# Expert weights handed over in order of use, loaded 2 MB and 4 MB at a time

## The chip, the cores and the metric

One Trainium2 chip, one core of it. The metric is the device time of one execution in microseconds; lower is better. The kernel before takes 1661.31 us (median of three runs, 1660.14 to 1664.47).

## The reference

A two-layer encoder trunk over 256 tokens of width 2048, all in float32. Layer 0 mixes tokens with a bidirectional mLSTM, layer 1 with multi-head latent attention. Each is followed by the same kind of expert stage, the part that the change touches:

```
gates = top 2 of the 4 experts of the best group, by sigmoid(x @ router_w)   # 16 experts, 4 groups
hg = x @ w_gate[e]          # (256, 2048) @ (2048, 512), for every expert e
hu = x @ w_up[e]            # the same shape
a  = silu(hg) * hu * gates[:, e]
y += a @ w_down[e]          # (256, 512) @ (512, 2048)
```

All 16 experts of a layer are read: 3 x 4 MB each, 201 MB a layer, 403 MB in all, out of some 534 MB that the whole kernel loads.

## The kernel before

**Stages.** Layer 0's mixer runs until about 414 us of the profiled span, its expert stage to 849 us, layer 1's mixer to 1217 us and its expert stage to the end.

**Units, pairs, steps.** Expert weights are counted in units of 1 MB: 128 partitions x 4 rows x 512 columns of float32, 8 KB in each partition. Experts are worked on in 8 pairs a layer; a pair has 24 units, numbered k = 24 i + n within the layer. TensorE multiplies both experts of a pair in turns, one in each half of the array, so that a step of 16 matmuls needs one unit of each expert: a pair is 12 steps, 8 of gate and up (L1173) and 4 of down (L1218). Units n = 0 to 15 are gate and up, 16 to 23 are down. The last pair's down projection goes by columns (L1237), from a tensor that the host lays out for it (`in_last_down`), units k = 184 to 191.

**The order within a load.** A load is one expert's 2 MB: 16 KB in a row for each partition, which is two units of the same expert. Units 0 and 1 are therefore expert e = 0, and 2 and 3 expert e = 1, while a step takes units 0 and 2, the next 1 and 3. The function `in_turn(k)` gives the place in the order of use: k // 4 * 4 + (0, 2, 1, 3)[k % 4].

**Places.** There are 23 places of 8 KB a partition for the first 23 units, and 18 of them are used again in a ring: `seat(k)` is (k - 4) % 18 for k from 34 on, and 0 to 10 for k = 23 to 33. A place of the first 23 units is one of 0 to 22; units 18 and 19 sit in 16 and 17, unit 22 in 11, and places 18 to 22 are not used again. `DOUBLE[s]` is the tile of two neighbouring places, s even. The last pair's units go to places of their own order (176 to 183 to 0 to 7, 184 to 191 to 10 to 17).

**The queue of loads.** SyncE issues all weight loads, in program order, on one queue. Before each it waits (`room`, L581) until the semaphore `unit_used` says that what was in the place has been multiplied; TensorE raises it by one for each unit, in the order of use. The loop at L633 issues the units k = 23 to 55 (`FINE` = 56) one by one, 1 MB each, sorted by when their place comes free; the loop at L636 issues k = 56 to 167 in order by 2 MB; the last pair's come by 1 MB again (L645), and its last two up units, 13 and 15 (`LAST_UPS`), by halves. Line 590 of the profile is `single` (1 MB), line 587 is `double` (2 MB).

**Waits of TensorE.** `arrived(n)` waits for the landing of unit n's load: for 2 MB loads at each even n.

Of the kernel before, what the change touches and what calls it, by code (L numbers as in the profile page):

```python
# [112 lines left out]
FINE = 56  # L113
# [3 lines left out]
LAST_UPS = (13, 15)  # L117


def in_turn(k):  # L120

    return k if k >= BY_COLUMNS else k // 4 * 4 + (0, 2, 1, 3)[k % 4]


def seat(k):


    if k >= BY_COLUMNS:
        return k - BY_COLUMNS + RING + 2
    if k >= BY_COLUMNS - RING:  # L130
        return k - BY_COLUMNS + RING
    if k == ALONE:
        return WIDE + ONCE
    if k == WIDE + ONCE:
        return ALONE
    if EARLY <= k < EARLY + ALONE:
        return k - EARLY
    return k if k < WIDE - 2 else k + 2 if k < WIDE else k - 2 if k < WIDE + 2 else k if k < EARLY else (k - ONCE) % WIDE
# [12 lines left out]
def split(u):  # L151

    k, singles = (u - U_MOE0, SINGLES[0]) if u < U_CKV else (u - U_MOE1, SINGLES[1])
    return expert(u) and (k in singles or k >= PAIRS * PAIR_UNITS - HALVES)


def places():

    slots, turns, held = [], [], [0] * EARLY

    for u in range(U_ALL):
        if u < U_MOE0:
            s = u % RING
        elif u < U_CKV:
            s = seat(u - U_MOE0)
        elif u < U_MOE1:
            s = (u - U_CKV) % RING
        else:
            k = seat(u - U_MOE1)
            s = (k + U_MOE1 - U_CKV) % RING if k < RING else k  # L170
        if not expert(u) or s % 2 == 0 or split(u):
            held[s] += 1
        slots.append(s)
        turns.append(held[s])
    return slots, turns
# [67 lines left out]
def trunk(nc, w, out):  # L243
# [8 lines left out]
    with ctx:  # L252
# [38 lines left out]
        DOUBLE = {}  # L291
        ring, LO = [], []
        for s in range(RING):
            here = top[0]
            if s % 2 == 0:
# [5 lines left out]
        DOUBLE[RING + 8] = sb("SPARE", [P, 2, UNIT_K, UNIT_C])  # L301
# [168 lines left out]
        def in_double(u):  # L470

            if PLACE[u] == WIDE + ONCE:
                return UNIT_ALONE[:, :, :]
            return DOUBLE[PLACE[u] // 2 * 2][:, PLACE[u] % 2, :, :]

        def gate_rows(layer):

            return (w[n][layer].rearrange("e (q p k) f -> e q p (k f)", p=P, k=2 * UNIT_K)
                    for n in ("moe_w_gate", "moe_w_up"))

        def down_rows(layer):

            return w["moe_w_down"][layer].rearrange("e (c p k) d -> e c p (k d)", p=P, k=2)

        def half(v, k):

            return v[:, UNIT_K * UNIT_C * k:UNIT_K * UNIT_C * (k + 1)]

        def expert_sources(wg, wu, wd, i):

            n, h = divmod(i, 2) if isinstance(i, int) else i
            for q in range(2):
                for m in (wg, wu):
                    for e in range(2):
                        yield m[PER_GRP * (2 * h + e) + n, q]
            for c in range(2):
                for e in range(2):
                    yield wd[PER_GRP * (2 * h + e) + n, c]
# [13 lines left out]
        def _(sp):  # L512
            used = sem("unit_used")

            def unit(u, src, i=0):
                if U_CKV <= u < U_CKV + RING:
                    sp.wait_ge(used, U_MOE0 + in_turn(last_in(PLACE[u])) + 1)
# [51 lines left out]
            def spare(layer, base):  # L569

                u = base + WIDE
                if layer:
                    sp.wait_ge(used, U_MOE0 + in_turn(last_in(PLACE[u] + 1)) + 1)
                src = list(expert_sources(*gate_rows(layer), down_rows(layer), 0))[WIDE // 2]
                sp.dma_start(flat4(DOUBLE[PLACE[u]]), src).then_inc(sem(f"unit_loaded_{PLACE[u]}"), 16)

            def experts(layer, base):
                wg, wu = gate_rows(layer)
                wd = down_rows(layer)

                def room(k, units):  # L581

                    last = max(in_turn(before_in_slot(k + n)) for n in range(units))
                    sp.wait_ge(used, base + last + 1)
# [8 lines left out]
                first = list(expert_sources(wg, wu, wd, 0))  # L593
# [29 lines left out]
                single(base + WIDE + ONCE, list(expert_sources(wg, wu, wd, 0))[(WIDE + ONCE) // 2])  # L623
# [8 lines left out]
                all_of = [src for i in range(PAIRS) for src in expert_sources(wg, wu, wd, i)]  # L632
                for k in sorted(range(EARLY, FINE), key=lambda k: in_turn(before_in_slot(k))):  # L633
                    room(k, 1)
                    single(base + k, all_of[k // 2])
                for i in range(PAIRS):  # L636
                    if i == MIDDLE:
                        sp.wait_ge(sem("over_done"), layer + 1)
                    for n in range(PAIR_UNITS // 2):
                        k = PAIR_UNITS * i + 2 * n  # L640
                        if FINE <= k < PAIRS * PAIR_UNITS - HALVES:
                            room(k, 2)
                            double(base + k, all_of[k // 2])
                front = PAIRS * PAIR_UNITS - PAIR_UNITS
                for k in sorted(range(PAIRS * PAIR_UNITS - HALVES, PAIRS * PAIR_UNITS), key=in_turn):  # L645
                    room(k, 1)
                    if k >= BY_COLUMNS:
                        d, c = divmod(k - BY_COLUMNS, 2)
                        sp.dma_start(in_double(base + k).rearrange("p k c -> p (k c)"), w["last_down"][layer, d, c])\
                            .then_inc(sem(f"unit_loaded_{PLACE[base + k]}"), 16)  # L650
                    elif k - front not in LAST_UPS:
                        single(base + k, all_of[k // 2])
                    elif k - front == LAST_UPS[-1]:
                        for h in range(2):
                            for n in LAST_UPS:
                                src = half(all_of[(front + n) // 2], n % 2)
                                rows = slice(2 * h, 2 * h + 2)
                                sp.dma_start(in_double(base + front + n)[:, rows, :].rearrange("p k c -> p (k c)"),
                                             src[:, 2 * h * UNIT_C:2 * (h + 1) * UNIT_C])\
                                    .then_inc(sem(f"unit_loaded_{PLACE[base + front + n]}" if h else "last_ups_begun"), 16)  # L660
# [40 lines left out]
            sp.wait_ge(used, U_MOE0 + max(in_turn(last_in(RING + n)) for n in range(2)) + 1)  # L701
# [28 lines left out]
        def _(pool):  # L730
# [7 lines left out]
            for l in range(2):  # L738
# [14 lines left out]
                wg, wu = gate_rows(l)  # L753
                wd = down_rows(l)
                with pool.If(flag > 0):
                    with pool.Fori(0, EXTRA) as q:
                        with pool.Fori(0, PER_GRP) as i:
                            with pool.Fori(0, 2) as h:
                                j = q * PAIRS + 2 * i + h
                                whole = list(expert_sources(wg, wu, wd, (i, h)))  # L760
                                srcs = [half(whole[2 * b + e], k) for b in range(PAIR_UNITS // 4) for k in range(2) for e in range(2)]
# [10 lines left out]
        def _(pe):  # L772
# [284 lines left out]
            def experts(l, base):  # L1057
                def order(n):

                    return n // 4 * 4 + 2 * (n % 2) + n // 2 % 2  # L1060

# [69 lines left out]
                def opening(m, g, arrived, slot, consumed, left_out=()):  # L1131
# [3 lines left out]
                    arrived(2)  # L1135
                    for c in range(UNIT_K):
                        for e in range(2):
                            last = pe.matmul(PS[64 * e:64 * e + 64, 0, :], tokens_of(c, e),
                                             slot(2 * e)[:, c, :], start=(c == 0), stop=False)
# [6 lines left out]
                def pair(m, j, g, following, arrived, slot, consumed, whole, prev, first=False, opened=False, late=False):  # L1146
# [7 lines left out]
                    for q in range(2):  # L1154
                        if first:
                            gather_some(m, g, (2 * q, 2 * q + 1), True)
                        for up in range(2):
                            for k in range(2):
                                if first and up == 0:
                                    pe.wait_ge(sem(m + "xg_ready"), 4 * g + 2 * q + k + 1)  # L1160
                                units = [8 * q + 4 * up + 2 * e + k for e in range(2)]
                                here = not (opened and q == up == k == 0)
                                in_two = whole and not following and units[0] == LAST_UPS[0]
                                if in_two:
                                    pe.wait_ge(sem("last_ups_begun"), 32 * (l + 1))
# [44 lines left out]
                    for c in range(FC):  # L1210
                        units = [16 + 4 * (c // 2) + 2 * e + c % 2 for e in range(2)]
# [40 lines left out]
                def overflow():  # L1252
# [3 lines left out]
                    with pe.Fori(0, EXTRA) as q:  # L1256
                        with pe.Fori(0, PAIRS) as i:
                            k = q * PAIRS + i
                            j, g = k + MIDDLE + LAYER_PAIRS * l, k + MIDDLE + 1 + LAYER_GATHERS * l
                            for d in range(4):  # L1260
# [3 lines left out]
                            pair(m, j, g, 0, lambda n: pe.wait_ge(sem(f"over_loaded_{l}_{order(n) % 4}"),  # L1264
                                                                  16 * (PAIR_UNITS // 4) * k + 16 * (order(n) // 4 + 1)),
                                 lambda n: OV[order(n) % 4], sem(f"over_free_{l}"), False, False)
# [555 lines left out]
        def _(dve):  # L1822
# [718 lines left out]
_WEIGHTS = ["x", "a_w_in", "a_w_out", "b_w_in", "b_w_ukv", "b_q_norm", "b_k_norm", "b_w_out",  # L2541
            "moe_w_gate", "moe_w_up", "moe_w_down"]
# [61 lines left out]

# [14 lines left out]
```

## Time and profile before

| | |
|---|---|
| median of three runs | 1661.31 us |
| the profiled execution's own time | 1661.03 us |
| its span | 1659.3 us |
| TensorE busy | 1611.1 us, 97% of the span |
| VectorE, ScalarE, GpSimd busy | 46%, 29%, 3% |
| loads and stores | 535.84 MB, mean 323 GB/s |
| mean granted TensorE clock | 0.996 of full speed |

The span runs from the first to the last instruction; the execution's own time lies 1.7 us above it. TensorE is nearly always busy, yet a share over the whole span says nothing of a single stage: in the expert stages the profile shows the DMA engines at 9 tenths or more in every slice, with 412 to 429 GB/s, and in the mixers at 150 to 300 GB/s. Issue to landing is the time from SyncE's issue of a load to its semaphore; where it is many times the duration of the transfer, the load has stood behind others.

### The profile page before, as it was taken

To read this page: it belongs to the slowest core of one execution; us is meant where nothing else is said; L and a number is where in the kernel's file an instruction comes from. 1 tells how busy PE (TensorE), PEld (TensorE's weight loads), DVE (VectorE), ACT (ScalarE), POOL (GpSimd) and SP (SyncE) were. 2 spreads that over 40 slices of the span, in tenths; PEclk is the share of its full clock that TensorE was granted. 3 is DMA by queue.
4 is the path that set the end of the run, shared out by engine and by line. 5 is a ranking of instruction groups with operands and counts; after the bars stand their busy time and mean duration, and the time that the engine had idled before them with its cause. 6 is when DMAs were issued, how large, how long until landed. Compare 5 with 4: busy or idle time off the path is not lost.

```text
span 1659.3 us, 19405 instructions
## 1 busy us (share of the span) xinstructions
PE 1611.1 (97%) x8014; PEld 1010.1 (61%) x8014; DVE 758.6 (46%) x1316; ACT 482.1 (29%) x622; POOL 44.9 (3%) x26
## 2 busy tenths in 40 slices
PE   9999999999999999889999999999999999989898
PEld 8888888887433434333459999888754344333343
DVE  5885477744332222212267777684532322222223
ACT  6444456434000000000054565564320000000000
POOL 0000000000000000000040000020000000000000
PEclk9999999999999999999999999999999999999999
DMA  9755656577999999999995545554799999999998
GB/s 368 268 189 166 198 166 197 171 264 298 421 415 425 428 427 427 428 429 425 420 360 174 152 137 158 190 179 151 290 423 421 423 427 428 428 427 428 427 422 342
DMA packets 110441, 535.84 MB, mean 323 GB/s; under 512 B 8704, under 2 KB 28048, under 8 KB 77840
## 3 DMA queue, kind: packets, MB, share of 16 engines
q1 hardware_dynamic: 109920, 534.04, 82.0%
q8 instruction: 66, 1.08, 0.3%
q10 hardware_dynamic: 432, 0.53, 0.1%
q14 instruction: 23, 0.19, 0.0%
HBM read 532.43 MB, written 2.11 MB: 322 GB/s over the span
## 4 chain that ended last, share of the span: by engine, by line
PE 81%; DMA 15%; DVE 2%; ACT 1%; SPq 1%; issue 1%; DVEq 0%; ACTq 0%
PE PS L806 33%; PE PS L1173 21%; PE PS L1218 8%; DMA DOUBLE<-in_moe_w_down 5%; DMA DOUBLE<-in_moe_w_up 5%; PE PS L927 2%; PE PS L1079 2%; DMA SPARE<-in_moe_w_gate 2%; PE PS L1237 2%; DMA OVD<-in_moe_w_gate 2%; PE PS L1116 2%; PE PS L1117 1%; PE PS L933 1%; DMA ring<-in_a_w_in 1%; PE PS L1099 1%; PE PS L1004 1%
## 5 line engine op out<-in xcount | busy, mean ns | idle before, releaser
L1173 PE MATMUL PS<-DOUBLE,AREA 128*64 128x512 f32 x1264 | 336.1, 597 | 10.8 <-DMA OVD<-in_moe_w_gate 5.4
L1834 DVE TENSOR_TENSOR LO<-ring,HI 128x2048 fp32r<-128x2048 f32 (+1 forms) x122 | 262.4, 2151 | 168.1 <-ACT HI L1459 167.6
L806 PE MATMUL PS<-HI,XT_BOTH 128*128 128x512 f32 (+1 forms) x1344 | 298.0, 373 | 1.1 <-issue 0.6
L1459 ACT ACTIVATE HI<-ring 128x2048 fp32r<-128x2048 f32 (+1 forms) x122 | 219.8, 1802 | 272.4 <-PE PS L806 234.5
L806 PEld LDWEIGHTS PS<-HI,XT_BOTH 128*128 128x128 f32 x1344 | 244.1, 188 | 35.5 <-issue 2.4
L1173 PEld LDWEIGHTS PS<-DOUBLE,AREA 128*64 128x64 f32 x1264 | 107.6, 139 | 196.0 <-issue 195.7
L1173 PE MATMUL PS<-OVD,AREA 128*64 128x512 f32 x400 | 179.2, 599 | 0.0
L806 PE MATMUL PS<-LO,XT_BOTH 128*128 128x512 f32 (+1 forms) x672 | 152.5, 368 | 0.0
L2243 DVE TENSOR_TENSOR AREA<-PS,SMALL 128x512 f32<-128x512 f32 x64 | 44.1, 689 | 236.3 <-PE PS L1079 203.0
L1218 PE MATMUL PS<-DOUBLE,AREA 128*64 128x512 f32 x528 | 143.4, 599 | 3.6 <-DMA DOUBLE<-in_moe_w_down 3.2
L1645 ACT ACTIVATE AREA<-PS 128x512 f32<-128x512 f32 x16 | 9.6, 597 | 438.7 <-PE PS L1173 438.7
L806 PEld LDWEIGHTS PS<-LO,XT_BOTH 128*128 128x128 f32 x672 | 122.9, 188 | 16.2
L2233 DVE TENSOR_TENSOR X<-PS,X 128x512 f32<-128x512 f32 x112 | 69.9, 682 | 122.1 <-PE PS L1117 122.1
L1655 ACT ACTIVATE Y_hi<-PS,AREA 128x512 fp32r<-128x512 f32 x64 | 44.0, 688 | 229.4 <-PE PS L1218 197.7
L2251 DVE SCALAR_TENSOR_TENSOR Y_lo<-PS,AREA,Y_hi 128x512 fp32r<-128x512 f32 x64 | 48.0, 750 | 107.1 <-ACT Y_hi L1655 102.3
L1218 PEld LDWEIGHTS PS<-DOUBLE,AREA 128*64 128x64 f32 x528 | 45.6, 137 | 69.3 <-issue 66.2
L1173 PEld LDWEIGHTS PS<-OVD,AREA 128*64 128x64 f32 x400 | 54.2, 139 | 44.2 <-issue 44.2
L1173 PE MATMUL PS<-SPARE,AREA 128*64 128x512 f32 x176 | 78.4, 593 | 0.5 <-DMA DOUBLE<-in_moe_w_gate 0.5
L1173 PE MATMUL PS<-WIDED,AREA 128*64 128x512 f32 x160 | 72.2, 596 | 0.8 <-DMA OVD<-in_moe_w_up 0.8
L1079 PEld LDWEIGHTS PS<-AREA,XN 128*128 128x128 f32 x448 | 47.9, 140 | 34.0 <-issue 34.0
L1218 PE MATMUL PS<-OVD,AREA 128*64 128x512 f32 x144 | 63.9, 595 | 3.3 <-DMA WIDED<-in_moe_w_down 3.3
L1079 PE MATMUL PS<-AREA,XN 128*128 128x128 f32 x448 | 61.2, 280 | 0.0
(325 smaller groups left out, 1847.3 us busy)
## 6 DMA issues: line engine op xcount, KB each, us to landing
DOUBLE<-in_moe_w_up SPq DMA_DIRECT2D x26, 2048.0 KB, 24.3
DOUBLE<-in_moe_w_gate SPq DMA_DIRECT2D x24, 2048.0 KB, 21.4
DOUBLE<-in_moe_w_down SPq DMA_DIRECT2D x24, 2048.0 KB, 28.5
ring<-in_a_w_in SPq DMA_DIRECT2D x47, 1024.0 KB, 5.2
DOUBLE<-in_moe_w_gate SPq DMA_DIRECT2D x30, 1024.0 KB, 13.3
DOUBLE<-in_moe_w_up SPq DMA_DIRECT2D x24, 1024.0 KB, 15.1
ring<-in_b_w_in SPq DMA_DIRECT2D x32, 768.0 KB, 4.4
OVD<-in_moe_w_up SPq DMA_DIRECT2D x9, 2048.0 KB, 29.1
```

Source lines behind the costliest of these rows:

```text
L806: mm = pe.matmul(PS[:, banks[t], 0:n], lhs(k0 + kk, t)[part], weights[:, kk, 0:n], start=first and kk == 0 and p == 0, stop=last and kk == ...
L927: pe.matmul(PS[:, 4 * (b % 2) + ch, :], HI[u % 2][:, kk, ch * P:(ch + 1) * P], XT_BOTH[:, :, k, :], start=k == 0, stop=False)
L1079: last = pe.transpose(PS[:, GATHER_BANKS[g] + k // 2, at_:at_ + P], XN[:, t, c * P:(c + 1) * P], m_["SEL"][:, t, :])
L1116: pe.matmul(PS[:, bank, :], SCT[:, t * P:(t + 1) * P], YH[:, d, :], start=True, stop=False)
L1173: last = pe.matmul(PS[64 * e:64 * e + 64, up, :], tokens_of(c, e), slot(units[e])[:, kk, :], start=(c == 0), stop=(c == DC - 1))
L1218: last = pe.matmul(PS[64 * e:64 * e + 64, 4 + d, :], m_["AT"][:, c, 64 * e:64 * e + 64], slot(units[e])[:, d, :], start=(c == 0), stop=(c ...
L1459: act.activation(HI[s % 2][:, :, 0:n], ring[PLACE[u]][:, :, 0:n], ACT.Copy).then_inc(sem("hi_ready"), 1)
L1655: act.activation(YH[:, d, :], PS[:, 4 + d, :], ACT.Copy, scale=m_["GS"])\
L1834: tt(LO[PLACE[u]][:, :, 0:n], ring[PLACE[u]][:, :, 0:n], HI[s % 2][:, :, 0:n], ALU.subtract)\
L2233: tt(xs, PS[:, bank, :], xs, ALU.add).then_inc(sem(counted), 1)
L2243: tt(m_["XG"][:, 4 * g:4 * g + 4, :].rearrange("p k (t s) -> p k t s", t=NT), PS[:, banks[g]:banks[g] + 2, :].rearrange("p b (k t s) -> p ...
L2251: stt(YL[:, d, :], PS[:, 4 + d, :], m_["GS"], YH[:, d, :], ALU.mult, ALU.subtract)\
```

## The change

The host lays out the expert weights in one tensor, `in_experts`, of shape (2 layers, 8 pairs, 6 blocks, 128 partitions, 32 KB). A block is four units in order of use: (first half, e = 0), (first half, e = 1), (second half, e = 0), (second half, e = 1). Two units that are used in one step are neighbours, in memory and in the place. `in_turn` is gone; the three expert tensors are no longer inputs. The bytes that are loaded, the matmuls and their order stay.

Pairs 4, 5 and 6 (k = 96 to 167) are loaded by 4 MB: 32 KB in a row for each partition, into four tiles of four neighbouring places, in turn. Their places 8 and 9 stay unused in these pairs. The tile SPARE moves to lie behind HI, so that one of the four is in one piece. `FINE` goes from 56 to 34: units 34 to 55 are loaded by 2 MB, in order, and not by 1 MB as places come free. Of the last pair, gate and up come by 2 MB (units 168 to 181), the last two ups still in two halves, now 1 MB for both experts together.

```diff
-FINE = 56
+FINE = 34
-LAST_UPS = (13, 15)
-def in_turn(k):
-    return k if k >= BY_COLUMNS else k // 4 * 4 + (0, 2, 1, 3)[k % 4]
+LAST_UPS = (14, 15)
+QUAD_PAIRS = (4, PAIRS - 1)
+QUAD_SEATS = ((4, 5, 6, 7), (12, 13, 14, 15), (10, 11, 16, 17), (0, 1, 2, 3))
+def quad(k):
+    return QUAD_PAIRS[0] * PAIR_UNITS <= k < QUAD_PAIRS[1] * PAIR_UNITS

 def seat(k):
+    if quad(k):
+        return QUAD_SEATS[(k - QUAD_PAIRS[0] * PAIR_UNITS) // 4 % 4][k % 4]
...
-        DOUBLE = {}
+        DOUBLE, QUAD = {}, {}
+        DOUBLE[RING + 8] = sb("SPARE", [P, 2, UNIT_K, UNIT_C])
+        QUAD[RING + 4] = at("QUADX", over_at - 2 * UNIT_K * UNIT_C * 4, [P, 4, UNIT_K, UNIT_C])
+        QUAD[RING + 2] = at("QUADH", over_at + 2 * UNIT_K * UNIT_C * 4, [P, 4, UNIT_K, UNIT_C])
...
+        def two_units(layer, i, n):
+            return half(w["experts"][layer, i, n // 2], 2 * (n % 2), 2)
...
                 def room(k, units):
-                    last = max(in_turn(before_in_slot(k + n)) for n in range(units))
+                    last = max(before_in_slot(k + n) for n in range(units))
                     sp.wait_ge(used, base + last + 1)
...
-                for k in sorted(range(EARLY, FINE), key=lambda k: in_turn(before_in_slot(k))):
+                for k in sorted(range(EARLY, FINE), key=before_in_slot):
                     room(k, 1)
                     single(base + k, all_of[k // 2])
                 for i in range(PAIRS):
...
-                        if FINE <= k < PAIRS * PAIR_UNITS - HALVES:
+                        if quad(k):
+                            if k % 4 == 0:
+                                room(k, 4)
+                                sp.dma_start(flat4(QUAD[PLACE[base + k]]), w["experts"][layer, i, n // 2])\
+                                    .then_inc(sem(f"unit_loaded_{PLACE[base + k]}"), 16)
+                        elif FINE <= k < PAIRS * PAIR_UNITS - HALVES:
                             room(k, 2)
                             double(base + k, all_of[k // 2])
...
-                for k in sorted(range(PAIRS * PAIR_UNITS - HALVES, PAIRS * PAIR_UNITS), key=in_turn):
+                for k in range(PAIRS * PAIR_UNITS - HALVES, BY_COLUMNS, 2):
+                    room(k, 2)
+                    if k - front != LAST_UPS[0]:
+                        double(base + k, all_of[k // 2])
...
-                                units = [8 * q + 4 * up + 2 * e + k for e in range(2)]
+                                units = [8 * q + 4 * up + 2 * k + e for e in range(2)]
...
-                        units = [16 + 4 * (c // 2) + 2 * e + c % 2 for e in range(2)]
+                        units = [16 + 2 * c + e for e in range(2)]
...
+def expert_rows(inputs):
+    gate, up, down = (np.asarray(inputs[n]) for n in ("moe_w_gate", "moe_w_up", "moe_w_down"))
+    rows = np.empty((2, PAIRS, PAIR_UNITS // 4, P, 2, 2, UNIT_K * UNIT_C), np.float32)
+    for i in range(PAIRS):
+        n, h = divmod(i, 2)
+        for e in range(2):
+            x = PER_GRP * (2 * h + e) + n
+            for q in range(2):
+                for at, a in ((2 * q, gate), (2 * q + 1, up), (4 + q, down)):
+                    rows[:, i, at, :, :, e] = a[:, x].reshape(2, 2, P, 2, -1)[:, q]
+    return rows.reshape(2, PAIRS, PAIR_UNITS // 4, P, 4 * UNIT_K * UNIT_C)
```

## Rows read from the trace of the kernel before

**Rows 1.** The page: its span, and its DMA row by slices.

```profile
span 1659.3 us, 19405 instructions
DMA  9755656577999999999995545554799999999998
```

**Rows 2.** Busy time by window, layer 1's pairs 2-3 and 4-5; columns named in the first row.

```profile
core 0: us, PE busy (x) PEld busy (x) DVE busy (x) ACT busy (x) POOL busy (x), PEclk, DMA share, GB/s
1358.00:1410.00 52.00, 51.57 (x254) 20.98 (x252) 13.79 (x25) 4.33 (x7) 0.00 (x0) 1.00 1.01 427
1462.00:1514.00 52.00, 46.17 (x218) 19.05 (x218) 12.24 (x21) 3.35 (x5) 0.00 (x0) 1.00 1.01 427
```

**Rows 3.** The chain that ended last, layer 1's expert stage: start, us, what.

```profile
1478.39 31.91 DMA DOUBLE<-in_moe_w_up
...
1517.52 31.93 DMA DOUBLE<-in_moe_w_up
...
1558.90 30.20 DMA DOUBLE<-in_moe_w_down
...
1589.23 7.09 PE PS L1218 x32
...
1608.70 15.21 DMA DOUBLE<-in_moe_w_up
```

**Rows 4.** The same chain, the end of layer 0's expert stage and what follows.

```profile
756.07 30.53 DMA DOUBLE<-in_moe_w_down
...
786.73 8.79 PE PS L1218 x32
...
818.07 10.58 PE PS L1173 x48
...
849.65 1.90 ACT HI L1459
```

**Rows 5.** SyncE's issues in time, layer 0; the last row is layer 1's counterpart.

```profile
455.48 3.76 SPq L590 DMA_DIRECT2D SPARE<-in_moe_w_up  x2
...
463.52 0.33 SPq L590 DMA_DIRECT2D OVD<-in_moe_w_gate  x1
...
470.35 0.80 SPq L590 DMA_DIRECT2D DOUBLE<-in_moe_w_down  x2
...
473.78 0.81 SPq L590 DMA_DIRECT2D DOUBLE<-in_moe_w_down  x2
...
479.26 0.80 SPq L590 DMA_DIRECT2D DOUBLE<-in_moe_w_down  x2
...
484.89 0.33 SPq L590 DMA_DIRECT2D DOUBLE<-in_moe_w_down  x1
...
1267.19 0.33 SPq L590 DMA_DIRECT2D OVD<-in_moe_w_gate  x1
```

**Rows 6.** Issue to landing of single loads, by tile: three issues of layer 0.

```profile
L590 SPq DMA_DIRECT2D OVD<-in_moe_w_up x1: 431/431/431, 449.6 to 449.6; - x1
DMA to landing us min/median/max: 15.0/15.0/15.0
...
L590 SPq DMA_DIRECT2D SPARE<-in_moe_w_up x1: 328/328/328, 458.9 to 458.9; - x1
DMA to landing us min/median/max: 10.7/10.7/10.7
...
L590 SPq DMA_DIRECT2D DOUBLE<-in_moe_w_down x2: 327/380/432, 470.3 to 470.7; - x2
DMA to landing us min/median/max: 6.7/7.7/8.8
```

**Rows 7.** Issue to landing of two 2 MB loads that met an idle queue.

```profile
L587 SPq DMA_DIRECT2D DOUBLE<-in_moe_w_gate x1: 328/328/328, 381.5 to 381.5; - x1
L587 SPq DMA_DIRECT2D DOUBLE<-in_moe_w_up x1: 327/327/327, 393.4 to 393.4; - x1
...
DMA to landing us min/median/max: 8.1/8.4/8.7
```

More of the change, by code:

```diff
@@ L153, in split, with in_quad @@
     k, singles = (u - U_MOE0, SINGLES[0]) if u < U_CKV else (u - U_MOE1, SINGLES[1])
-    return expert(u) and (k in singles or k >= PAIRS * PAIR_UNITS - HALVES)
+    return expert(u) and (k in singles or k >= BY_COLUMNS)
+def in_quad(u):
+    return expert(u) and quad(u - U_MOE0 if u < U_CKV else u - U_MOE1)
 def places():
@@ L170, in places @@
             s = (k + U_MOE1 - U_CKV) % RING if k < RING else k
-        if not expert(u) or s % 2 == 0 or split(u):
+        if in_quad(u):
+            held[s] += 1 if u % 4 == U_MOE0 % 4 else 0
+        elif not expert(u) or s % 2 == 0 or split(u):
             held[s] += 1
@@ L294, in trunk @@
             here = top[0]
+            if s % 4 == 0:
+                QUAD[s] = at(f"QUAD{s}", here, [P, 4, UNIT_K, UNIT_C])
             if s % 2 == 0:
@@ L300, in trunk @@
         DOUBLE[WIDE + 2] = at(f"DOUBLE{WIDE + 2}", x_at, [P, 2, UNIT_K, UNIT_C])
-        DOUBLE[RING + 8] = sb("SPARE", [P, 2, UNIT_K, UNIT_C])
         SMALL = sb("SMALL", [P, SMALL_W])
@@ L473, in in_double, with half @@
                 return UNIT_ALONE[:, :, :]
+            if in_quad(u):
+                return QUAD[PLACE[u - (u - U_MOE0) % 4]][:, (u - U_MOE0) % 4, :, :]
             return DOUBLE[PLACE[u] // 2 * 2][:, PLACE[u] % 2, :, :]
[L476 to L498, printed above, removed]
+        def half(v, k, n=1):
+            return v[:, UNIT_K * UNIT_C * k:UNIT_K * UNIT_C * (k + n)]
+        def two_units(layer, i, n):
+            return half(w["experts"][layer, i, n // 2], 2 * (n % 2), 2)
         def stream(s):
@@ L516, in unit @@
                 if U_CKV <= u < U_CKV + RING:
-                    sp.wait_ge(used, U_MOE0 + in_turn(last_in(PLACE[u])) + 1)
+                    sp.wait_ge(used, U_MOE0 + last_in(PLACE[u]) + 1)
                 elif u >= RING:
@@ L572, in spare @@
                 if layer:
-                    sp.wait_ge(used, U_MOE0 + in_turn(last_in(PLACE[u] + 1)) + 1)
-                src = list(expert_sources(*gate_rows(layer), down_rows(layer), 0))[WIDE // 2]
-                sp.dma_start(flat4(DOUBLE[PLACE[u]]), src).then_inc(sem(f"unit_loaded_{PLACE[u]}"), 16)
+                    sp.wait_ge(used, U_MOE0 + last_in(PLACE[u] + 1) + 1)
+                sp.dma_start(flat4(DOUBLE[PLACE[u]]), two_units(layer, 0, WIDE // 2)).then_inc(sem(f"unit_loaded_{PLACE[u]}"), 16)
             def experts(layer, base):
-                wg, wu = gate_rows(layer)
-                wd = down_rows(layer)
                 def room(k, units):
-                    last = max(in_turn(before_in_slot(k + n)) for n in range(units))
+                    last = max(before_in_slot(k + n) for n in range(units))
                     sp.wait_ge(used, base + last + 1)
@@ L591, in single @@
                         .then_inc(sem(f"unit_loaded_{PLACE[u]}"), 16)
-                first = list(expert_sources(wg, wu, wd, 0))
+                first = [two_units(layer, 0, n) for n in range(PAIR_UNITS // 2)]
                 def early(k):
@@ L622, in experts @@
                 early_half(11)
-                single(base + WIDE + ONCE, list(expert_sources(wg, wu, wd, 0))[(WIDE + ONCE) // 2])
+                early_half(WIDE + ONCE)
                 if layer == 0:
@@ L631, in experts @@
                 early(WIDE + 2)
-                all_of = [src for i in range(PAIRS) for src in expert_sources(wg, wu, wd, i)]
-                for k in sorted(range(EARLY, FINE), key=lambda k: in_turn(before_in_slot(k))):
+                all_of = [two_units(layer, i, n) for i in range(PAIRS) for n in range(PAIR_UNITS // 2)]
+                for k in sorted(range(EARLY, FINE), key=before_in_slot):
                     room(k, 1)
@@ L644, in experts @@
                 front = PAIRS * PAIR_UNITS - PAIR_UNITS
-                for k in sorted(range(PAIRS * PAIR_UNITS - HALVES, PAIRS * PAIR_UNITS), key=in_turn):
-                    room(k, 1)
[L647 to L660, printed above, removed]
+                for k in range(PAIRS * PAIR_UNITS - HALVES, BY_COLUMNS, 2):
+                    room(k, 2)
+                    if k - front != LAST_UPS[0]:
+                        double(base + k, all_of[k // 2])
+                    else:
+                        src = all_of[k // 2].rearrange("p (e k) -> p e k", e=2)
+                        for h in range(2):
+                            rows = slice(2 * h, 2 * h + 2)
+                            sp.dma_start(DOUBLE[PLACE[base + k]][:, :, rows, :].rearrange("p e k c -> p e (k c)"),
+                                         src[:, :, 2 * h * UNIT_C:2 * (h + 1) * UNIT_C])\
+                                .then_inc(sem(f"unit_loaded_{PLACE[base + k]}" if h else "last_ups_begun"), 16)
+                for k in range(BY_COLUMNS, PAIRS * PAIR_UNITS):
+                    room(k, 1)
+                    d, c = divmod(k - BY_COLUMNS, 2)
+                    sp.dma_start(in_double(base + k).rearrange("p k c -> p (k c)"), w["last_down"][layer, d, c])\
+                        .then_inc(sem(f"unit_loaded_{PLACE[base + k]}"), 16)
             a_in = k_view(w["a_w_in"][0])
@@ L700, in _ @@
                 unit(U_CKV + n, b_in[n][:, :, Q_COLS:Q_COLS + RANK])
-            sp.wait_ge(used, U_MOE0 + max(in_turn(last_in(RING + n)) for n in range(2)) + 1)
+            sp.wait_ge(used, U_MOE0 + max(last_in(RING + n) for n in range(2)) + 1)
             sp.dma_start(b_["WKR"], w["b_w_in"][0].rearrange("(c p) n -> p c n", p=P)[:, :, Q_COLS + RANK:])\
@@ L752, in _ @@
                 flag = pool.value_load(FLAG[0:1, l:l + 1], min_val=0, max_val=1)
-                wg, wu = gate_rows(l)
-                wd = down_rows(l)
                 with pool.If(flag > 0):
@@ L759, in _ @@
                                 j = q * PAIRS + 2 * i + h
-                                whole = list(expert_sources(wg, wu, wd, (i, h)))
-                                srcs = [half(whole[2 * b + e], k) for b in range(PAIR_UNITS // 4) for k in range(2) for e in range(2)]
+                                srcs = [half(two_units(l, 2 * i + h, n // 2), n % 2) for n in range(PAIR_UNITS)]
                                 for n, src in enumerate(srcs):
@@ L1057, in experts @@
             def experts(l, base):
-                def order(n):
-                    return n // 4 * 4 + 2 * (n % 2) + n // 2 % 2
                 def gather(m, j, groups=range(4), first=False, chunks_of=range(4), low_of=None):
@@ L1134, in opening @@
                     arrived(0)
-                    arrived(2)
+                    arrived(1)
                     for c in range(UNIT_K):
@@ L1138, in opening @@
                             last = pe.matmul(PS[64 * e:64 * e + 64, 0, :], tokens_of(c, e),
-                                             slot(2 * e)[:, c, :], start=(c == 0), stop=False)
+                                             slot(e)[:, c, :], start=(c == 0), stop=False)
                             if c == UNIT_K - 1:
@@ L1164, in pair @@
                                 if in_two:
-                                    pe.wait_ge(sem("last_ups_begun"), 32 * (l + 1))
+                                    pe.wait_ge(sem("last_ups_begun"), 16 * (l + 1))
                                 for n in units if here and not in_two else ():
@@ L1263, in overflow @@
                             gather_some(m, g)
-                            pair(m, j, g, 0, lambda n: pe.wait_ge(sem(f"over_loaded_{l}_{order(n) % 4}"),
-                                                                  16 * (PAIR_UNITS // 4) * k + 16 * (order(n) // 4 + 1)),
-                                 lambda n: OV[order(n) % 4], sem(f"over_free_{l}"), False, False)
+                            pair(m, j, g, 0, lambda n: pe.wait_ge(sem(f"over_loaded_{l}_{n % 4}"),
+                                                                  16 * (PAIR_UNITS // 4) * k + 16 * (n // 4 + 1)),
+                                 lambda n: OV[n % 4], sem(f"over_free_{l}"), False, False)
                     gather(m, gather_turn(l, MIDDLE), (0, 1))
@@ L2538, in _ @@
             experts(1)
-_WEIGHTS = ["x", "a_w_in", "a_w_out", "b_w_in", "b_w_ukv", "b_q_norm", "b_k_norm", "b_w_out",
-            "moe_w_gate", "moe_w_up", "moe_w_down"]
+_WEIGHTS = ["x", "a_w_in", "a_w_out", "b_w_in", "b_w_ukv", "b_q_norm", "b_k_norm", "b_w_out"]
 def constants():
@@ L2602, in laid_out @@
     }
+def expert_rows(inputs):
+    import numpy as np
+    gate, up, down = (np.asarray(inputs[n]) for n in ("moe_w_gate", "moe_w_up", "moe_w_down"))
[8 more added lines that the diff above has]
+    return rows.reshape(2, PAIRS, PAIR_UNITS // 4, P, 4 * UNIT_K * UNIT_C)
 def kernel(**inputs):
@@ L2612 @@
     arrays.update(laid_out(inputs))
+    arrays["in_experts"] = expert_rows(inputs)
     arrays["in_last_down"] = down_blocks(inputs)
```

## The prediction, made before the result was known

> **What bounds the kernel now.** I read the page first: TensorE is busy for 97% of the span, but the DMA row shows two stretches of nines, and these are the expert stages [rows 1]. So the second view is busy time by window. In layer 1's pairs 2 to 3 TensorE works for 51.57 of 52 us and the DMA engines show a share of 1.01 at 427 GB/s; in pairs 4 to 5 the DMA row is the same and TensorE is down to 46.17 us [rows 2]. The loads never pause, TensorE does: a pair's 24 MB take longer to arrive than to be multiplied, the 23 units loaded ahead are used up by the fourth pair, and from there the stage goes at the pace of the queue.
>
> The third view, the chain, gives that pace. The long waits in layer 1 end with landings: 1478.39 + 31.91 = 1510.30, then 1549.45, 1589.10 and 1608.70 + 15.21 = 1623.91 [rows 3]. By the order of units these are the landings of the unit counts 136, 152, 168 and 182 (count 136: units 0 to 135 are there). 136 to 152 is 8 loads of 2 MB in 39.15 us: 4.89 us each, back to back. 168 to 182 is 14 loads of 1 MB in 34.81 us: 2.49 us each, so 4.97 for two. The waits also stand in layer 0, where the chain ends at 756.07 + 30.53 = 786.60 (count 168) [rows 4]. The rest of each stage hangs on these landings. What counts is thus only when the DMA queue delivers units 168 to 184; a TensorE wait taken away earlier comes back later.
>
> **Two units in order instead of four out of order.** A step now needs one 2 MB load and not two. In pairs 1 to 3 no wait on a load stands in the chain, so nothing is gained there; in pairs 4 to 6 a load is 4 MB, and the count that must have landed is again a multiple of four; in the last pair two 1 MB loads in turn order were as fine as one 2 MB load is. Price 0. It could only be worth something if the queue had slack, and it has none [rows 2]. The new order of freeing is the same too: before, units 0 and 2 came free in one step, now 0 and 1.
>
> **1 MB loads become 2 MB loads.** Units 34 to 55 are 11 pairs of loads, 168 to 181 are 7. Each saves 4.97 - 4.89 = 0.08 us of the queue: 0.9 us before count 168 and 0.6 us after it, in each layer.
>
> **2 MB loads become 4 MB loads.** 18 a layer. No row shows one. From 8 KB to 16 KB a row the queue won 0.08 us on 2 MB; if a row of any length costs the same extra, 4 MB win 0.08 us again: 9.70 for 9.78. That gives 18 x 0.08 = 1.5 us a layer. Bounds: 0 if the row of 16 KB is already at the port's pace, 3 us if the saving per load doubles instead, and 1.5 us of loss if one long row blocks as much as it saved before. I take 1.5, the value nearest to the row. The Trainium skill, DMA: Bandwidth & Descriptors, "Where 436 GB/s comes from", gives 435.2 GB/s as the ports' ceiling; by it 4 MB take no less than 9.64 us and the 18 loads could save 2.6 us at most. The trace, at 428.8 GB/s for 2 MB, agrees with a ceiling close by.
>
> The four tiles are refilled when their own four units are used. The tightest is the second, units 100 to 103, whose places were last held by units 88 to 91. TensorE uses unit 24 at 470.35 [rows 5] and needs at most 52 us a pair [rows 2], so unit 91 is used by about 470.35 + 67 / 24 x 52 = 615.5; count 100 lands at 786.60 - 34 x 4.89 = 620.3 at the earliest, later by the hole below. The issue comes in time, and later ones lie further ahead. Nothing is lost there.
>
> **FINE = 34, the term that goes the other way.** Before, the single loads follow whatever place comes free. Look at the issues between 455 and 471 us [rows 5]: unit 38 at 455.48, 39 at 458.92 (both SPARE), unit 51 at 463.52 (place 11, freed by unit 22, far ahead of its turn), then unit 40, and 41 and 43 at 470.35. After the change, units 38 and 39 go as one load at 458.92, when place 17 is free. The next in order is the load of units 40 and 41 into places 0 and 1. Place 0 held unit 23, place 1 unit 24, and 24 is used in the first step of pair 1 only: the issue of 470.35 [rows 5]. Unit 51 waits for its neighbour 50. So between 458.92 and 470.35 nothing is issued.
>
> How full is the queue then? The issue of 449.6 (count 38) lands at 464.6, that of 458.9 (count 40) at 469.6, and the two of 470.3 and 470.7 (43 and 44) at 477.0 and 479.5 [rows 6]: 2.49 us apart throughout, so the queue before just held, with the last landing 4 us behind the issue. After: count 38 lands at 464.4 (two of its loads are 2 MB now), count 40 at 469.3, and the queue is empty a microsecond before anything new is issued. A 2 MB load that met an idle queue took 8.1 to 8.7 us to land [rows 7]. So count 42 lands at 470.35 + 8.4 = 478.75 where a full queue would give 469.3 + 4.9 = 474.2: a hole of 4.5 us. The next loads are issued at 473.8, 479.3 and 484.9 [rows 5], while the queue then holds to 483.6 and 488.5; with 8.4 us each they make it, the last one barely. After that the places are aligned and issues run ahead. Bounds: 1.1 us if a start from idle cost nothing, 5.5 us if the first is 8.7 and the load of 484.9 slips by 0.7. The Trainium skill, the same page, "Anatomy of one DMA", gives a lone DMA 2.0 us plus bytes over 436 GB/s, 6.8 us for 2 MB; by it the hole would be 3.0 us. The two rows at 8.1 and 8.7 differ from it, though measured beside other work.
>
> Can it be caught up? No: the queue has no slack afterwards [rows 2, 3]. Layer 1 issues at the same distance (1267.19 for 463.52, pair 0 being 803.67 us later) [rows 5], so it has the same hole.
>
> **The sum.** Count 168 lands later by 4.5 - 0.9 - 1.5 = 2.1 us in each layer. In layer 1 the ups of the last pair bind (count 182), 0.6 us earlier: +1.5. In layer 0 the 32 matmuls after the wait take 8.79 us where layer 1 shows 7.09 [rows 3, 4], and TensorE comes to the ups at 818.07 + 10.58 / 3 = 821.6, 34.9 us after the landing, against 34.2 for seven 2 MB loads: TensorE binds, and layer 0 is +2.1. ScalarE's first split of the next stage (849.65) follows at once [rows 4], so the shift is handed on. Together +3.6 us on the profiled execution's 1661.03 (span 1659.3): 1664.6. The median of the runs is 1661.31, 0.3 higher; I say 1664.9.
>
> **Rivals.** A change under 0.3% (5 us) can't be told from none for this kernel.
>
> (a) No hole: the queue is fuller than my ledger says, or it restarts at no cost. For it: the before is seamless at the same place, and 1.1 us is a possible price. Against: 11.4 us without an issue with 4 MB queued. Then layer 0 wins 0.9 + 1.5 and layer 1 3.0: -5.4 us, 1655.9, faster. 20%.
>
> (b) The slow side: 4 MB loads bring nothing, since 16 KB rows are at the port's pace, and the hole stands. It costs 1.5 us more in each layer: +6.6, 1667.9. It decides from the point where a 4 MB load takes more than about 9.74 us. For it: nothing in the trace shows a faster pace than 429 GB/s. Against: the step from 1 MB to 2 MB did gain. The Trainium skill, the same page, "Rules for kernel authors", is content with 1 MB a DMA for full bandwidth; the trace's 0.08 us between 1 and 2 MB is small but there. The same time comes out if the hardware cuts the 32 KB rows in two. 28%.
>
> (c) The finer order does let TensorE through: if half of TensorE's idle time of the last three pairs of both layers went, by the window of pairs 4 to 5 (52 - 46.17) x 6 / 2 = 17 us [rows 2], the time would be 1644. Against it stands the DMA share of 1.01 while TensorE waits [rows 2]. 5%.
>
> My forecast with its own bounds (1661 to 1667.5) has 47%.
>
> Range 1655.5 to 1669.5: it takes in (a) and (b), and leaves out (c) and a hole of over 5 us together with lossy 4 MB loads. Faster by over 0.3%: 19% (14 of (a), all of (c)); slower: 35% ((b), and 7 of the forecast, its upper edge); same: 46%.
>
> **What would show it.** Right: by window, a DMA share well under 1 around 469 to 473 us and 1273 to 1277 us; an issue gap at SyncE from 458.9 to 470.35; one landing of 8 to 9 us there with nothing before it; landings 9.70 us apart in pairs 4 to 6; the last wait on ups ending near 1627.5 us in layer 1. Wrong: a DMA share of 1.01 in these windows, or 9.78 us and more for 4 MB, or TensorE idle before the ups gone.

## The result, and the profile after

The changed kernel takes 1664.65 us (median of 19 runs) beside 1661.88 us for the kernel before (19 runs in the same sessions): a ratio of 1.0017, 95% interval 1.001 to 1.0025, so 2.8 us slower. That is within what I had called no change, but with 19 runs the interval leaves out 1: the loss is small and real. The forecast was 1664.9. The profiled execution's span is 1662.2 us, 2.9 us more than before [rows 1]; its page:

```profile
span 1662.2 us, 19256 instructions
DMA  9755656577989999999995545554799999999998
```

The DMA row is the one of before [rows 1] but for one digit: slice 12 (457 to 499 us) has an 8 where there was a 9. By window (columns as in [rows 2]), layer 0 and then layer 1:

```profile
460.00:466.00 6.00, 6.00 (x31) 2.08 (x31) 1.22 (x2) 1.08 (x2) 0.00 (x0) 1.00 1.01 429
466.00:472.00 6.00, 6.00 (x30) 2.02 (x28) 2.76 (x6) 1.67 (x3) 0.00 (x0) 1.00 0.23 68
1264.00:1270.00 6.00, 6.00 (x32) 2.23 (x31) 0.92 (x2) 0.78 (x2) 0.00 (x0) 1.00 1.03 434
1270.00:1276.00 6.00, 6.00 (x30) 2.02 (x28) 3.05 (x6) 1.97 (x3) 0.00 (x0) 1.00 0.32 131
```

This is the hole: a share of 0.23 and 68 GB/s between stretches at the full pace, while TensorE, with some 16 MB in store (40 units landed, 24 used), works all of the 6 us and notices nothing. The issues around it in layer 0, the timeline of SyncE, answering to [rows 5]:

```profile
459.30 0.33 SPq L586 DMA_DIRECT2D SPARE<-in_experts  x1
...
470.74 0.33 SPq L586 DMA_DIRECT2D DOUBLE<-in_experts  x1
```

There is none between, as the order of places said. Issue to landing of the same two loads and of the next two, answering to [rows 6]:

```profile
L586 SPq DMA_DIRECT2D SPARE<-in_experts x1: 327/327/327, 459.3 to 459.3; - x1
DMA to landing us min/median/max: 9.3/9.3/9.3
...
L586 SPq DMA_DIRECT2D DOUBLE<-in_experts x1: 328/328/328, 470.7 to 470.7; - x1
DMA to landing us min/median/max: 7.4/7.4/7.4
...
L586 SPq DMA_DIRECT2D DOUBLE<-in_experts x1: 328/328/328, 474.2 to 474.2; - x1
DMA to landing us min/median/max: 10.2/10.2/10.2
...
L586 SPq DMA_DIRECT2D DOUBLE<-in_experts x1: 328/328/328, 479.7 to 479.7; - x1
DMA to landing us min/median/max: 9.9/9.9/9.9
```

Count 40 lands at 468.6 and count 42 at 478.1: 9.5 us apart where a full queue has 4.9, a hole of 4.6 us. In layer 1 the same loads, issued at 1263.6 and 1275.0, land at 1274.6 and 1282.2: 7.6 us apart, a hole of 2.7 us only, since count 40 lands 56.0 us after the stage's start there and 54.4 us after it in layer 0. And the chain in layer 1, answering to [rows 3] (start, us, what):

```profile
1481.39 33.21 DMA QUADX<-in_experts
...
1521.79 31.57 DMA QUADX<-in_experts
...
1562.78 29.50 DMA QUADX<-in_experts
...
1592.33 7.09 PE PS L1215 x32
...
1606.35 20.21 DMA DOUBLE<-in_experts
```

The landings are 1514.60, 1553.36, 1592.28 and 1626.56 us, for the counts 136, 152, 168 and 182 as before. 136 to 168 is 8 loads of 4 MB in 77.68 us: 9.71 each; 168 to 182 is 7 loads of 2 MB in 34.28 us: 4.90 each. The same in layer 0, answering to [rows 4]:

```profile
759.74 28.44 DMA QUADX<-in_experts
...
788.22 7.09 PE PS L1215 x32
...
802.25 20.20 DMA DOUBLE<-in_experts
...
850.66 1.90 ACT HI L1456
```

To set the stages side by side one needs their starts, the first gather of each; the chain before, and after:

```profile
413.89 3.79 PE PS L1099 x32
...
1217.56 3.79 PE PS L1099 x32
```

```profile
414.28 3.79 PE PS L1096 x32
...
1218.58 3.79 PE PS L1096 x32
```

Of the 2.9 us of span, 0.39 lie ahead of the first expert stage (the change has no part in it: the two profiled executions differ by it), 0.63 between the starts of the two stages (804.30 for 803.67), and 1.88 behind the second start.

### The profile page after: what moved, and what is told of

The parts are those of the page before. It is cut to its first block, busy times and chain, and to the rows that moved or that the text cites. A ratio compares the mean times of both kernels' runs of the same rounds, so it can differ in the third digit from the quotient of the medians.

```text
span 1662.2 us, 19256 instructions
## 1 busy us (share of the span) xinstructions
PE 1610.9 (97%) x8014; PEld 1003.1 (60%) x8014; DVE 758.7 (46%) x1316; ACT 482.1 (29%) x622; POOL 44.9 (3%) x26
## 4 chain that ended last, share of the span: by engine, by line
PE 76%; DMA 19%; DVE 2%; ACT 1%; SPq 1%; issue 1%; DVEq 0%; ACTq 0%
PE PS L807 33%; PE PS L1170 18%; DMA QUADX<-in_experts 10%; PE PS L1215 8%; DMA QUAD<-in_experts 6%; PE PS L928 2%; DMA DOUBLE<-in_experts 2%; PE PS L1234 2%; PE PS L1113 1%; PE PS L934 1%; PE PS L1076 1%; PE PS L1114 1%; DMA ring<-in_a_w_in 1%; PE PS L1096 1%; PE PS L1005 1%; PE PS L1370 1%
## 5 line engine op out<-in xcount | busy, mean ns | idle before, releaser
L1170 PE MATMUL PS<-DOUBLE,AREA 128*64 128x512 f32 x848 | 191.8, 595 | 2.1 <-DMA DOUBLE<-in_experts 2.1
L1170 PEld LDWEIGHTS PS<-DOUBLE,AREA 128*64 128x64 f32 x848 | 60.6, 138 | 118.4 <-issue 111.2
L1170 PE MATMUL PS<-QUAD,AREA 128*64 128x512 f32 x352 | 78.7, 596 | 3.9 <-DMA QUAD<-in_experts 3.9
L1215 PE MATMUL PS<-DOUBLE,AREA 128*64 128x512 f32 x304 | 71.2, 596 | 0.3
L2275 DVE TENSOR_TENSOR AREA<-PS,AREA 128x512 f32<-128x512 f32 x16 | 16.9, 1058 | 95.3 <-PE PS L1170 95.3
L1170 PE MATMUL PS<-OVD,AREA 128*64 128x512 f32 x224 | 57.7, 593 | 0.0
L1170 PEld LDWEIGHTS PS<-QUAD,AREA 128*64 128x64 f32 x352 | 25.2, 138 | 53.4 <-issue 44.4
L1113 PE MATMUL PS<-Y_hi,SCT 128*128 128x512 f32 x124 | 52.6, 424 | 0.0
L1170 PE MATMUL PS<-QUADH,AREA 128*64 128x512 f32 x192 | 45.1, 616 | 6.7 <-DMA QUADH<-in_experts 6.7
```

Of the source, the lines that this page charges most:

```text
L1113: pe.matmul(PS[:, bank, :], SCT[:, t * P:(t + 1) * P], YH[:, d, :], start=True, stop=False)
L1170: last = pe.matmul(PS[64 * e:64 * e + 64, up, :], tokens_of(c, e), slot(units[e])[:, kk, :], start=(c == 0), stop=(c == DC - 1))
L1215: last = pe.matmul(PS[64 * e:64 * e + 64, 4 + d, :], m_["AT"][:, c, 64 * e:64 * e + 64], slot(units[e])[:, d, :], start=(c == 0), stop=(c ...
```

## The experiments

Each ran in five rounds beside the kernel before; ratios are to it, with 95% intervals. The changed kernel's 1664.65 us comes from other sessions, so where a median is set against it the ratios (its own is 1.0017) are the safer comparison. Medians of before in these sessions: 1661.57 us for the first four, 1661.43 us for the other three. My theory was the prediction's: in the expert stages the time goes by the DMA queue, the change makes it run dry once a layer, and larger loads give a part of that back. The rivals: the 4 MB loads or the new layout cost the time; or the hole is harmless and made up for later.

### FINE back at 56

```diff
-FINE = 34
+FINE = 56
```

> The changed kernel with FINE back at 56: units 34 to 55 are loaded one by one, as places come free; order of use, 4 MB loads and the last pair's 2 MB loads stay. Theory (the straddling 2 MB load of units 40 and 41 leaves the queue empty from 468 to 471 us, 6 us of landings lost by count 44 in each layer): unit 40 is issued with unit 51 at about 467 again and the queue is nearly seamless; 11 pairs of loads cost 0.08 us more each. Per layer -6 + 1 (a short hole is left, since in the order of use units 22 and 23 come free together) + 0.9, so about -4 us a layer: ratio to before near 0.997, some 1656 us where the changed kernel has 1664.65. DMA share 466 to 472 us near 1 instead of 0.23. Rival (4 MB loads or the new layout cost the time, the hole is made up for later): the time stays at 1664 to 1667, ratio 1.002 to 1.003, though the hole is gone.

Measured: 1658.08 us, ratio 0.9981 (0.9972 to 0.999): 6.6 us under the changed kernel (6.0 by the ratios) where I expected about 8, and faster than before. One number undone turns the loss into a gain; the hole binds and isn't made up for. It isn't gone altogether. By window, and SyncE's issues there:

```profile
460.00:466.00 6.00, 6.00 (x29) 2.06 (x30) 1.40 (x2) 1.26 (x2) 0.00 (x0) 1.00 1.01 419
466.00:472.00 6.00, 6.00 (x30) 2.03 (x28) 2.58 (x6) 1.49 (x3) 0.00 (x0) 1.00 0.80 306
```

```profile
459.08 0.80 SPq L589 DMA_DIRECT2D SPARE<-in_experts  x2
467.12 0.33 SPq L589 DMA_DIRECT2D OVD<-in_experts  x1
467.49 0.43 SPq L589 DMA_DIRECT2D DOUBLE<-in_experts  x1
```

Here 8 us pass without an issue; before, units 38 and 51 went at 455.48 and 463.52 [rows 5]. In the order of use units 18 and 19 are finished in one step and so are 22 and 23, so their places come free together.

### No 4 MB loads

```diff
-QUAD_PAIRS = (4, PAIRS - 1)
+QUAD_PAIRS = (PAIRS - 1, PAIRS - 1)
```

> The changed kernel without 4 MB loads: pairs 4 to 6 by 2 MB into the ring of 18 places, all else as changed. Theory: 9.70 us for 4 MB against 2 x 4.89 = 9.78: 18 loads, 1.5 us a layer, so +3 us: about 1667.5, ratio to before 1.0035. Rival (4 MB loads cost time, as they are issued late or need four places): faster than the changed kernel, ratio under 1.0017. The hole at 468 to 471 us stays the same in both.

Measured: 1667.57 us, ratio 1.0044 (1.003 to 1.0058), 2.9 us above the changed kernel (4.5 by the ratios, from five runs). The rival that blames the 4 MB loads falls. The two rates in the same window of 52 us in pairs 5 and 6, first without and then, in the changed kernel, with 4 MB loads:

```profile
705.00:757.00 52.00, 45.83 (x222) 17.37 (x220) 11.26 (x20) 3.94 (x6) 0.00 (x0) 1.00 1.01 427
```

```profile
705.00:757.00 52.00, 46.73 (x221) 19.38 (x221) 13.52 (x24) 3.94 (x6) 0.00 (x0) 0.97 1.01 432
```

### Two-unit loads into places that come free together

Unit 23 goes to place 10, units 24 to 33 by 2 MB to 0 to 9, 40 and 41 to 10 and 11. Unit 23's load is now issued behind those of units 24 to 33.

```diff
+TURN_SEATS = (10, 0, 2, 4, 6, 8, 12, 14, 16)
+    if k == EARLY:
+        return ALONE - 1
-    if EARLY <= k < EARLY + ALONE:
-        return k - EARLY
+    if EARLY < k < FINE:
+        return k - EARLY - 1
+    if FINE + 6 <= k < QUAD_PAIRS[0] * PAIR_UNITS:
+        return TURN_SEATS[(k - FINE - 6) // 2 % 9] + k % 2
...
```

> The changed kernel with other places for units 23 to 95, so that every 2 MB load falls into two places that come free in one step: unit 23 goes to place 10, units 24 to 33 by 2 MB to 0 to 9, 40 and 41 to 10 and 11 (freed at 467 us instead of 470.4), then the ring in that order. Units 24 to 33 are 2 MB loads now too. Theory: the hole shrinks to 1 to 2 us, 0.4 us more from five pairs of loads: about -5 us a layer, 1654 to 1656, ratio to before 0.996. Rival (the hole does not bind): within 2 us of the changed kernel, ratio 1.001 to 1.002.

Measured: 1657.25 us, ratio 0.9977 (0.9967 to 0.9986); 7.4 us under the changed kernel (6.6 by the ratios) where I expected about 10. So it is the straddling of two steps, and not the size of 2 MB, that opened the long hole. What is left of it, in layer 0 and in layer 1:

```profile
466.00:472.00 6.00, 6.00 (x30) 2.03 (x28) 2.58 (x6) 1.49 (x3) 0.00 (x0) 1.00 0.74 270
...
1264.00:1270.00 6.00, 6.00 (x30) 1.99 (x32) 1.44 (x2) 1.36 (x2) 0.00 (x0) 1.00 0.92 352
1270.00:1276.00 6.00, 6.00 (x32) 2.01 (x30) 2.53 (x5) 1.39 (x3) 0.00 (x0) 1.00 0.72 262
```

That is 6 x 0.26 = 1.6 us in layer 0, as expected, and 6 x (0.08 + 0.28) = 2.2 us in layer 1, little more. Where the rest of the gain stayed is open.

### The hole alone, in the kernel before

```diff
-FINE = 56
+FINE = 34
```

> The kernel before with FINE = 34 alone: old layout, old order, no 4 MB loads; units 34 to 55 by 2 MB in order. Theory: the same hole appears at 468 to 472 us, since the 2 MB load of units 40 and 41 needs unit 24 used: count 56 lands 4 us later in each layer, so +8 us: about 1669.5, ratio 1.005. Rival (the hole comes from the order of use, not from FINE): the 2 MB loads save 0.9 us a layer and nothing is lost, ratio 0.999.

Measured: 1669.63 us, ratio 1.0055 (1.0041 to 1.0069): 8.1 us slower, in the old layout and the old order. By window, and SyncE's issues:

```profile
466.00:472.00 6.00, 6.00 (x32) 2.02 (x30) 2.48 (x5) 1.37 (x2) 0.00 (x0) 1.00 0.33 90
472.00:478.00 6.00, 6.00 (x38) 2.97 (x36) 1.72 (x3) 0.00 (x0) 0.00 (x0) 1.00 0.92 380
```

```profile
458.92 0.33 SPq L587 DMA_DIRECT2D SPARE<-in_moe_w_up  x1
470.35 3.76 SPq L587 DMA_DIRECT2D DOUBLE<-in_moe_w_down  x2
```

The same two issue times as in the prediction, and the same gap. FINE makes the hole without any other part of the change, and the rival that blames the order of use falls.

### The places that come free spread over four steps

Units 16 and 18 in the places that are not used again, 17 and 19 in those of the ring, 21 against 20 and 22 likewise. Units 16 to 22 come one by one for this; after them 1 MB loads up to unit 51.

```diff
+FIRST_SEATS = {16: 18, 17: 16, 18: 19, 19: 17, 20: 20, 21: ALONE, 22: 21, ALONE: WIDE + ONCE}
-    if k == ALONE:
-        return WIDE + ONCE
-    if k == WIDE + ONCE:
-        return ALONE
+    if k in FIRST_SEATS:
+        return FIRST_SEATS[k]
-FINE = 34
+FINE = 52
...
```

> Order of use, 4 MB loads and the last pair's 2 MB loads as changed; units 23 to 51 by 1 MB as places come free (FINE = 52), and of the first units 16 and 18 sit in the places that are not used again, 17 and 19 in the ones of the ring, likewise 20 and 22 against 21: so a place comes free in each of the steps at 455, 459, 463 and 467 us and not in two of them only. Theory: with FINE = 56 alone (1658.1) the queue still ran short once, DMA share 0.80 from 466 to 472 us; here the share is 1 throughout, and 1 to 1.5 us a layer are won: 1655 to 1656, ratio to before 0.9965. Rival (the rest of the gap at FINE = 56 is not the queue's): no faster than 1658, ratio 0.998.

Measured: 1656.64 us, ratio 0.9964 (0.9951 to 0.9978), the fastest of all. By window, and SyncE's issues:

```profile
460.00:466.00 6.00, 6.00 (x30) 2.00 (x29) 1.41 (x3) 1.37 (x2) 0.00 (x0) 1.00 1.01 422
466.00:472.00 6.00, 6.00 (x32) 2.02 (x30) 2.48 (x5) 1.37 (x2) 0.00 (x0) 1.00 1.01 401
```

```profile
455.49 3.76 SPq L589 DMA_DIRECT2D SPARE<-in_experts  x2
463.53 0.33 SPq L589 DMA_DIRECT2D OVD<-in_experts  x1
466.96 4.19 SPq L589 DMA_DIRECT2D DOUBLE<-in_experts  x3
```

The issues stand where they stood before [rows 5], and the share is 1.01. The time is in the forecast's place by the ratio, 0.6 us above it by the median. Against FINE = 56 alone the step is 1.4 us with overlapping intervals: that the last of the gap costs something is likely, not shown.

### The hole in one layer only

```diff
-FINE = 34
+FINE = (56, 34)     # by layer
...
```

> The changed kernel with FINE = 56 in layer 0 and 34 in layer 1. Theory (a hole in the queue costs in its own layer what it is long, and both layers add up): half of the 6.6 us between the changed kernel and FINE = 56 in both: 1661.4, ratio to before 1.000. Rival (layer 0 ends at TensorE's pace and hands its time on or not; only layer 1's hole counts): no gain, 1664.6, or all of it, 1658.

Measured: 1663.58 us, ratio 1.0004 (0.9993 to 1.0015). The middle between the two ratios, 0.9981 and 1.0017, is 0.9999, inside the interval. All of the gain (0.9981, at most 0.999) is outside it, so layer 1's hole counts. But the times don't rule out that it keeps none of the gain: 1.0017 has an interval of its own from 1.001 up, which overlaps, and the runs scatter from 1660.5 to 1666.8 us. The profile decides for layer 0. The starts of the two stages:

```profile
414.77 3.79 PE PS L1096 x32
...
1215.98 5.92 PE PS L1096 x32
```

They lie 801.21 us apart, in the changed kernel 804.30: layer 0 hands on 3.1 us when its long hole is short. (The second gather took 5.92 us for 3.79 because the granted clock was 0.61 of full speed there.) The windows show one short and one long gap:

```profile
466.00:472.00 6.00, 6.00 (x32) 2.02 (x30) 3.25 (x6) 2.06 (x3) 0.00 (x0) 1.00 0.81 309
...
1270.00:1276.00 6.00, 6.00 (x32) 2.02 (x30) 3.28 (x6) 2.44 (x4) 0.00 (x0) 1.00 0.15 63
```

### The order of use alone

```diff
-FINE = 34
+FINE = 56
-QUAD_PAIRS = (4, PAIRS - 1)
+QUAD_PAIRS = (PAIRS - 1, PAIRS - 1)
-                    room(k, 2)
                     if k - front != LAST_UPS[0]:
-                        double(base + k, all_of[k // 2])
+                        for n in range(2):
+                            room(k + n, 1)
+                            single(base + k + n, all_of[k // 2])
...
```

> Only the layout and the order of use: FINE = 56, no 4 MB loads, the last pair by 1 MB (its last two ups in halves of both experts). The prediction priced the order at 0. Theory now: units 18 and 19 come free in one step, and 22 and 23, so the queue runs short by 1 to 1.5 us a layer: +2 to +3 us on the kernel before, 1664, ratio 1.0015. Rival (the order costs nothing): ratio 1.000. Rival (a step that needs one load and not two lets TensorE start earlier): under 0.999.

Measured: 1662.12 us, ratio 1.0007 (0.9997 to 1.0016), with the short gap in the queue:

```profile
466.00:472.00 6.00, 6.00 (x30) 2.02 (x28) 2.62 (x6) 1.54 (x3) 0.00 (x0) 1.00 0.79 303
```

No gain from one load a step instead of two: rival (c) of the prediction, 17 us, is out. By the ratio a cost of 1.2 us (-0.5 to 2.7), less than I expected and not told from none. The step from here to FINE = 56 with all large loads, 1.0007 to 0.9981, is 4.3 us; the prediction's terms for 4 MB loads (3.0) and the last pair's 2 MB loads (1.2) give 4.2. With an interval of about 1 us or more on either ratio the closeness is no proof of each term.

## Why the prediction was right, and where not

**The bound.** Right: it was the DMA queue's pace, and a gap of a few us at its start was paid for at the end, although TensorE waited for no load for some 160 us after it (until 631 us in layer 0, 1435 us in layer 1). The hole put into the kernel before, and taken out of the changed one, both moved the time by it.

**The hole.** 4.5 us forecast, 4.6 in layer 0. The lone load landed earlier than the two of before had (7.4 us, not 8.4 [rows 7]), but the queue had also run dry 0.7 us sooner, count 40 landing at 468.6 and not 469.3. Then the next load came late too: issued at 474.2, it landed at 484.4, 6.3 us after its forerunner. I had left 0.7 us for such a slip and at a later load; it was 1.4. Whether the dry queue caused the slip is not shown: landings 1.0 to 1.6 us late also stand where the queue was full, as in the kernel before at 555.0 us, 5.9 us behind its forerunner at 549.1, with 18 us from issue to landing. In layer 1 the hole was 2.7 us, count 40 was 0.8 us late before it and a later load 1.4 us (issued at 1289.6). What the hole cost is best seen where both kernels are in step again: against the stage's start, count 56 lands 4.2 us later than before in layer 0 (99.7 for 95.4 us) and 3.8 in layer 1 (99.3 for 95.5), forecast 4.5 - 0.9 = 3.6. What slows the first loads after a dry queue no run shows. The 6.8 us that the prediction works out from the Trainium skill (DMA: Bandwidth & Descriptors, "Anatomy of one DMA") rests on a fit for loads that GpSimd issues; here SyncE issues, and the loads took 7.2 and 7.4 us.

**Larger loads.** 4.90 us for 2 MB against 4.89 forecast, and 9.71 us for 4 MB against 9.70: the saving read off 1 and 2 MB held for 4. The rows weren't cut in two either: the trace has 4608 packets of 32 KB, 128 for each of the 36 loads. The port ceiling of 435.2 GB/s that the Trainium skill gives (DMA: Bandwidth & Descriptors, "Where 436 GB/s comes from") is not touched: 4 MB in 9.71 us is 432 GB/s.

**The order of use, priced at 0.** The sentence that "the new order of freeing is the same" is wrong. It looked at units 0 and 2, whose places are both used again. Of units 16 to 23 only four (18, 19, 22, 23) sit in places of the ring, and the order of use frees these in two steps instead of four: 8 us without an issue even at FINE = 56. In the changed kernel the long hole hides this; alone it costs about 1 us by the ratio, which is within its interval of nothing.

**The two layers.** Against the stage's start, count 168 lands later by (1592.28 - 1218.58) - (1589.10 - 1217.56) = 2.16 us in layer 1 (forecast 2.1), and count 182 by 407.98 - 406.35 = 1.63 us (forecast 1.5). In layer 0 it is (788.18 - 414.28) - (786.60 - 413.89) = 1.19 us, and the next stage starts 0.63 us later, where I had 2.1. That is the step that failed, and it has two parts. The smaller, some 0.6 us, is in the last pair: I took the slow 32 matmuls after the wait (8.79 us, [rows 4]) as lasting, so that TensorE would bind. (They put TensorE at the ups 35.0 us after the landing, not 34.9, which changes nothing.) They were slow by the clock of one execution. The same 32 matmuls in the kernel before, layer 1 and then layer 0:

```profile
1589.23:1596.32 7.09, 7.09 (x34) 2.97 (x36) 1.60 (x3) 2.06 (x3) 0.00 (x0) 1.00 1.02 422
786.73:795.52 8.79, 8.79 (x34) 3.44 (x36) 1.60 (x3) 2.06 (x3) 0.00 (x0) 0.81 1.02 423
```

The granted clock was 0.81 of full speed there, and 8.79 x 0.81 = 7.1: for some 3 us it stood at its lower level (0.50 from 787.4 to 790.6 us). After the change it was 1.00, the matmuls took 7.09 us, TensorE waited for the load of 802.25 + 20.20 = 822.45, and the last pair's saving counted in layer 0 as in layer 1. The clock column of the window would have told this before.

The larger part, 0.9 us, is there at count 168 already. Between counts 56 and 168 some landings came late with the queue full: in the kernel before 3.3 us in sum in layer 0 and 2.0 in layer 1, after the change 1.5 in each. This favours the changed kernel by 1.8 and 0.5 us, and no term of the sum has it. So the 2.16 us of layer 1 are close to the forecast in part by luck: the hole with its slip cost more than I had put, and late landings of the other execution made up for it. What makes a landing late, and how often it happens, no run tells.

**The sum.** +3.6 us forecast, +2.8 by the medians, +2.9 by the spans. The mechanism and the signs of the terms hold, the order of use aside; that the sum lies within 1 us owes something to errors that cancel, as above.

## What to carry to other kernels

Where a stage goes by its DMA queue, the time is lost in the queue's emptiest moment, which lay here 160 us before the first wait on a load behind it. List the loads' issue times against the landings before them, and look where the two come together. A larger load waits for the last of its places, not the first: check when that one comes free, and count which freed places are really used again. How much that matters depends on how far the issues run ahead. The load of units 40 and 41 straddled two steps where the queue held two loads, and it ran dry; the 4 MB loads need the places of two steps as well, but are mostly issued some 20 us before the load ahead of them lands, and lost nothing. And before taking an odd duration as lasting, look at the granted clock in its window.

## What the runs showed of the hardware

- In an unbroken queue a load of 1 MB in rows of 8 KB takes 2.49 us, 2 MB in rows of 16 KB 4.89, 4 MB in rows of 32 KB 9.71: one load instead of two saves 0.08 us at the first doubling and 0.07 at the second.
- A 2 MB load that meets a queue gone dry lands 7.2 to 8.7 us behind its issue, 2.3 to 3.8 us more than its transfer. Against the landing before it the load was issued 0.4 us later for 7.2 us, 2.1 us later for 7.4, 3.8 us later for 8.7, but 1.0 us earlier for 8.1: these four show no plain order by how long the queue stood idle.
- A single landing comes 1.0 to 1.6 us late now and then, in full queues too (555.0 us in the kernel before), and the landings behind it stay late by as much.
- The granted clock fell to half for some 3 us, 0.7 us after TensorE went on from a wait of 2.7 us (787.4 to 790.6 us, kernel before), and 32 matmuls took 8.79 us instead of 7.09. At the same place in layer 1, and in both layers after the change, it stayed at full speed; the window from 705 to 757 us of the changed kernel, with 0.97, holds such a stretch elsewhere.
